# Norms behind three output projections taken in halves of the tokens, and an opening that waits for each x tile by itself

## The chip, the cores and the metric

One core of a Trainium2 chip runs the whole program. The metric is the device time of one execution in microseconds, taken as the median of the runs shown. Times inside an execution come from one profiled execution and count from the start of its span.

## The reference

Two transformer stages over one batch of 512 tokens of width 1024, all in float32. The first stage is a hybrid layer; the second has two layers whose norms are scaled and shifted by a vector computed from a condition, with an FFN that has a three-tap convolution over the tokens. For this change these lines matter (the second stage's norms have the form `norm(x) * (1 + scale) + shift`, and its branches are multiplied by a gate row before they are added):

```python
def rms_norm(x, g):
    x32 = x.astype(jnp.float32)
    y = x32 * lax.rsqrt(jnp.mean(x32 * x32, axis=-1, keepdims=True) + EPS) * g.astype(jnp.float32)
...
x = x + 0.5 * swiglu(rms_norm(x, ffn1_norm), ffn1_w_in, ffn1_w_out)
...
x = x + mix @ w_mix_out
x = x + 0.5 * swiglu(rms_norm(x, ffn2_norm), ffn2_w_in, ffn2_w_out)
```

## The kernel before

**Numbers.** Each float32 operand is split into a high and a low float32r part, and each product is made of three matmuls: high by high, low by high, high by low (`feature_major`, L344 to L346, and `token_major`, L350 to L352). Weights come in chunks of up to 128 x 2048, in two slots that alternate: SP loads `raw` (`load`, L340), ScalarE writes `w_hi` (`split_hi`, L323), VectorE writes `w_lo` (`split_lo`, L327). Chunks are numbered through the program. ScalarE may write `w_hi` of a chunk only when TensorE has used up the chunk two before it; SP may load a chunk when VectorE has split the one two before it.

**Order of work.** Each engine runs one list of instructions in program order, written out by hand in the blocks at the end of the file; semaphores join them. Stages: `norm_ffn1`, `ffn1`, `norm_mix`, the mixer's projection, attention, `out_1`; `norm_ffn2`, `ffn2`; then twice a layer of projection, attention, output projection (`out_2`, `out_3`), norm and FFN (`ffn3`, `ffn4`); a final norm.

**Norm.** `x` lies as four token tiles of 128 x 1024. For each, `stats_act` (L589, L591) squares and sums on ScalarE and takes the root, `scale_dve` (L597, L599) scales on VectorE into another tile, and TensorE transposes it in 128 x 128 blocks (L671) into PSUM. One PSUM bank holds feature tile t of all 512 tokens, so the bank is complete only with the last token tile. ScalarE then writes `xT_hi` (L617; with a shift L624 and L627) and VectorE `xT_lo` (L643; with a shift L646, and L654 for the odd tiles' scaling). `part(t)` lets a reader wait for feature tile t.

**FFN.** The hidden width is done in two halves of 11 tiles. In each there are ten tiles in pairs of slots (a pair is a gate tile and an up tile, 48 matmuls of 512 columns, one chunk), one single tile, and then the output matmuls in four chunks for each half of the columns, accumulated by token tile in banks 4 to 7. The halves and the pairs are loops. The first tile of a pair waits for `part(kt)` of the norm. After a pair, VectorE multiplies and splits the result (L902, L905). In `ffn1` VectorE also computes the modulation vector, eight steps (L546) for every two pairs, from weights that POOL loads into four slots; each step frees a slot for the next load. `ffn3` and `ffn4` apply the convolution (L832, L894).

**MixOut.** Two panels of 512 output columns; each has two chunks (pieces) of four k-tiles, and each piece goes over the four token tiles with 12 matmuls for each. A panel is done piece by piece: all tokens of piece 0, then all tokens of piece 1, so the token tiles become complete within the last 48 matmuls. VectorE adds the tiles to `x` as they complete (L2092, with a gate row L2094 and L2097) and scales the one before. The next FFN's first chunk is split by the FFN's predecessor in the ordinary order, ahead of the last adds. Between the panels of `out_2` stand the transposes and copies of a gate row (L2030, L2036, L2037) and on VectorE and ScalarE the sines and cosines (`rope_dve`, L2181 to L2194; `rope_act`, L2198).

**Opening.** SP loads the norm's vector, the four x tiles (one semaphore, x_in, that must reach 64), the first chunk, some 30 small vectors (`constants_load`, L377) and then the other chunks. TensorE transposes the vectors (`constants_pe`, L449 to L452, into banks 2 and 3) behind the norm's tile 3 and ahead of the first pair. VectorE copies them (`constants_dve`, L471 to L473) and makes two bias strips (L477 to L491), which POOL stores (`strips_store`) after six panels of modulation weights.

## Time and profile before

| | |
|---|---|
| median of 3 runs | 2290.57 us (2290.14 to 2291.48) |
| the profiled execution's own time | 2297.45 us |
| its span | 2295.9 us |
| mean granted clock of TensorE | 0.984 |
| TensorE idle, 2295.9 - 2219.4 busy | 76.5 us |
| ScalarE and VectorE busy | 952.0 and 1270.2 us |
| SP's issues of the small vectors, first to last | 4.15 to 19.3 us |
| ScalarE, the longest chunk's w_hi; VectorE, its w_lo | 1.9 and 2.29 us |

How to read it: an engine's row says when an instruction began and how long it was busy. Instructions of TensorE overlap, so the distance between two starts is the pace, and the duration shown is longer. "Idle before" names what ended the engine's wait. A granted clock of 1 is 2.4 GHz and 0.5 is 1.2 GHz; a number between is a mean over the stretch.

### The profile page before, as it was taken

How to read it: one execution, taken by the hardware profiler on the slowest of the kernel's cores; microseconds unless marked ns; L12 is line 12 of the kernel's file. 1: busy time of each engine (PE TensorE's matmuls, PEld its weight loads, DVE VectorE, ACT ScalarE, POOL GpSimd, SP SyncE). 2: the span in 40 equal slices, each digit the busy share in tenths (PEclk: the TensorE clock that was granted, in tenths of full speed). 3: DMA queues.
4: the chain of work that ended last, by engine and by line, in shares of the span. 5: the costliest groups of instructions: out<-in, count | busy, mean ns of one | idle time of the engine just before them, and what ended most of it. 6: DMA issues, size and time to landing. Idle time of an engine off the chain costs nothing.

```text
span 2295.9 us, 31127 instructions
## 1 busy us (share of the span) xinstructions
PE 2219.4 (97%) x11504; PEld 1829.6 (80%) x11504; DVE 1270.2 (55%) x2069; ACT 952.0 (41%) x1464; POOL 266.7 (12%) x442
## 2 busy tenths in 40 slices
PE   7999999998999999999999999999989999999998
PEld 5888887977778888887878788888878887888886
DVE  5754764455743363355347666456376755644554
ACT  4222223356734323324237454244254755533542
POOL 2110220034400020011027000000000430000000
PEclk9999999998999999999999999999999999999999
DMA  7863983231033274264221232332312212323332
GB/s 232 278 221 111 317 300 96 92 103 38 11 110 93 85 254 140 77 233 142 92 91 44 74 105 78 111 99 73 103 46 83 65 38 73 91 92 100 91 96 87
DMA packets 259489, 267.97 MB, mean 117 GB/s; under 512 B 9111, under 2 KB 202174, under 8 KB 259406
## 3 DMA queue, kind: packets, MB, share of 16 engines
q1 hardware_dynamic: 237677, 188.25, 27.6%
q0 software_dynamic: 21728, 78.63, 10.1%
q8 instruction: 50, 0.82, 0.1%
q14 instruction: 34, 0.27, 0.0%
HBM read 263.62 MB, written 12.66 MB: 120 GB/s over the span
## 4 chain that ended last, share of the span: by engine, by line
PE 88%; DVE 5%; ACT 4%; POOL 1%; issue 1%; DMA 1%; DVEq 0%; SPq 0%; ACTq 0%; POOLq 0%
PE bank L344 16%; PE bank L345 16%; PE bank L346 15%; PE bank L350 11%; PE bank L351 11%; PE bank L352 11%; PE bank L1571 2%; PE bank L1546 2%; PE bank L1522 2%; POOL probs L1729 1%; ACT probs L1607 1%; DVE w_lo L327 1%; DVE xT_lo L646 1%; PE bank L671 1%; PE bank L1945 0%
## 5 line engine op out<-in xcount | busy, mean ns | idle before, releaser
L327 DVE TENSOR_TENSOR w_lo<-raw,w_hi 128x2048 fp32r<-128x2048 f32 (+3 forms) x202 | 415.5, 2057 | 377.3 <-ACT w_hi L323 374.6
L344 PE MATMUL bank<-xT_hi,w_hi 128*128 128x512 f32 x1560 | 609.9, 391 | 5.1 <-DVE xT_lo L646 4.3
L345 PE MATMUL bank<-xT_lo,w_hi 128*128 128x512 f32 x1560 | 608.0, 390 | 0.0
L346 PE MATMUL bank<-xT_hi,w_lo 128*128 128x512 f32 x1560 | 607.8, 390 | 0.0
L323 ACT ACTIVATE w_hi<-raw 128x2048 fp32r<-128x2048 f32 (+3 forms) x202 | 348.2, 1724 | 485.7 <-PE bank L352 430.8
L344 PEld LDWEIGHTS bank<-xT_hi,w_hi 128*128 128x128 f32 x1560 | 292.7, 188 | 72.3 <-DVE xT_lo L646 8.2
L346 PEld LDWEIGHTS bank<-xT_hi,w_lo 128*128 128x128 f32 x1560 | 292.7, 188 | 62.1
L345 PEld LDWEIGHTS bank<-xT_lo,w_hi 128*128 128x128 f32 x1560 | 292.8, 188 | 60.3
L350 PE MATMUL bank<-w_hi,hid_hi 128*128 128x512 f32 x704 | 277.8, 395 | 0.0
L351 PE MATMUL bank<-w_lo,hid_hi 128*128 128x512 f32 x704 | 277.8, 395 | 0.0
L352 PE MATMUL bank<-w_hi,hid_lo 128*128 128x512 f32 x704 | 277.7, 395 | 0.0
L1729 POOL TENSOR_SCALAR probs<-probs,stat 128x256 f32<-128x256 f32 (+2 forms) x120 | 113.6, 958 | 726.6 <-DVE stat L1642 696.2
L840 ACT ACTIVATE hid_hi<-act_u 128x512 f32 (+1 forms) x88 | 55.6, 632 | 296.0 <-DVE act_u L902 296.0
L352 PEld LDWEIGHTS bank<-w_hi,hid_lo 128*128 128x128 f32 x704 | 132.7, 188 | 31.0
L350 PEld LDWEIGHTS bank<-w_hi,hid_hi 128*128 128x128 f32 x704 | 132.6, 188 | 31.0
L351 PEld LDWEIGHTS bank<-w_lo,hid_hi 128*128 128x128 f32 x704 | 132.7, 188 | 30.9
L1607 ACT ACTIVATE probs<-probs,small 128x512 f32<-128x512 f32 (+2 forms) x224 | 120.9, 542 | 63.6 <-DVE small L1671 63.6
L894 DVE SCALAR_TENSOR_TENSOR act_u<-bank,cols,act_u 128x511 f32<-128x511 f32 x88 | 65.9, 749 | 79.2 <-ACT act_u L832 72.8
L350 PE MATMUL bank<-w_hi,xT_hi 128*128 128x512 f32 (+2 forms) x288 | 102.5, 356 | 3.0 <-DVE xT_lo L646 2.9
L832 ACT ACTIVATE act_u<-bank,cols 128x512 f32<-128x512 f32 x44 | 34.3, 780 | 166.3 <-PE bank L346 166.3
L905 DVE TENSOR_TENSOR hid_lo<-act_u,hid_hi 128x512 f32 (+1 forms) x88 | 60.9, 692 | 76.0 <-ACT hid_hi L840 76.0
L351 PE MATMUL bank<-w_lo,xT_hi 128*128 128x512 f32 (+2 forms) x288 | 101.3, 352 | 0.0
(306 smaller groups left out, 2845.4 us busy)
## 6 DMA issues: line engine op xcount, KB each, us to landing
raw<-in_ffn_w_in_dram SPq DMA_DIRECT2D x40, 1024.0 KB, 6.2
raw<-in_f_win_dram SPq DMA_DIRECT2D x40, 1024.0 KB, 6.1
mod_w<-in_mod_w_dram POOLq DMA_DIRECT2D x48, 512.0 KB, 5.4
mod_w_more<-in_mod_w_dram POOLq DMA_DIRECT2D x48, 512.0 KB, 5.8
raw<-in_ffn_w_out_dram SPq DMA_DIRECT2D x24, 768.0 KB, 4.5
raw<-in_f_wout_dram SPq DMA_DIRECT2D x24, 768.0 KB, 4.4
raw<-in_a_wqkv_dram SPq DMA_DIRECT2D x12, 1024.0 KB, 5.2
skewed_strips<-bias_strips POOLq DMA_DIRECT2D x32, 320.0 KB, 6.6
```

Of the source, the lines that this page charges most:

```text
L323: act.activation(w_hi[:, slot, :n], raw[:, slot, :n], ACT.Copy).then_inc(hi_done, 1)
L327: dve.tensor_tensor(out=w_lo[:, slot, :n], in0=raw[:, slot, :n], in1=w_hi[:, slot, :n].bitcast(f32), op=ALU.subtract).then_inc(lo_done, 1)
L344: pe.matmul(o, lhsT=w[0], rhs=xs[0], start=first, stop=False)
L345: pe.matmul(o, lhsT=w[0], rhs=xs[1], start=False, stop=False)
L346: return pe.matmul(o, lhsT=w[1], rhs=xs[0], start=False, stop=last)
L350: pe.matmul(o, lhsT=xs[0], rhs=w[0], start=first, stop=False)
L351: pe.matmul(o, lhsT=xs[0], rhs=w[1], start=False, stop=False)
L352: return pe.matmul(o, lhsT=xs[1], rhs=w[0], start=False, stop=last)
L894: dve.scalar_tensor_tensor(out=dst[:, u, shift:], in0=bank[b][:, :SEQ - shift], scalar=w, in1=dst[:, u, shift:], op0=ALU.mult, op1=ALU.add ...
L905: dve.tensor_tensor(out=hid[1], in0=act_u[:, u, :], in1=hid[0].bitcast(f32), op=ALU.subtract).then_inc(pair_free[u], 1)
L1607: act.activation(p, p, ACT.Exp, scale=-1.0, bias=self.least(k, i), accum_out=self.sums(k, i)).then_inc(self.e, 1)
L1729: return engine.tensor_scalar(p, p, self.inverses(k, i), None, ALU.mult)
```

## The change

In the opening each x tile gets a semaphore of its own; ScalarE runs one square root on a constant first (`root_table`); the second chunk of weights is loaded ahead of the small vectors; eight extra 128 x 128 matmuls stand in front of the last feature tile's transposes of the first norm; the vectors' transposes move behind pair 0 of `ffn1` and into banks 4 and 5, their copies in front of pair 0's product on VectorE, and the strips' work into the first output stage (`strips_dve`).

The norms behind `out_1`, `out_2` and `out_3` become `HalfNorm`. The last panel is done in the order: piece 0 and piece 1 of token tiles 0 and 1, piece 0 of tiles 2 and 3, the transposes of tiles 0 and 1, piece 1 of tiles 2 and 3. A bank then holds two feature tiles of 256 tokens. ScalarE and VectorE write `xT_hi` and `xT_lo` for half the tokens at a time (`half_act`, `half_dve`). The FFN's pair 0 is done in two parts of 256 columns (`by_halves`), with the second half's transposes between them. The first FFN chunk is split between the statistics of tiles 0, 1 and half 0; its second chunk's w_hi (`second_split`) comes in front of half 1. In `out_2` the panel's second chunk is split ahead of the sines, and `modulate_for` comes ahead of the last panel's adds. The loops over an FFN's halves are written out, with pairs 0 and 1 of the first half ahead of the loop.

The core of the diff (the changes of counters, of calls and of the loops' frames are left out):

```diff
-        in_dma, x_in, first_in, small_in = sem("in_dma"), sem("x_in"), sem("first_in"), sem("small_in")
+        in_dma, first_in, small_in = sem("in_dma"), sem("first_in"), sem("small_in")
+        x_in = [sem(f"x_in{s}") for s in range(TOK)]
...
-            pe.transpose(bank[3][:, 0:P], rows[:, 4, :], ident[:, :])
+                pe.transpose(bank[4][:, b * P:(b + 1) * P], rows[:, b, :], ident[:, :])
+            pe.transpose(bank[5][:, 0:P], rows[:, 4, :], ident[:, :])
...
+        def strips_dve(dve):
             dve.wait_ge(small_in, 16 * SMALL_INS)
...
+        def first_tiles_dve(dve):
+            constants_dve(dve)
+            dve.wait_ge(cond_done, 1)
...
+        def root_table(act):
+
+            act.wait_ge(lo_done, 2)
+            act.activation(stat[:, 0:1], eps[:, :], ACT.Sqrt)
...
+                    if self.n == 0 and t == KT - 1:
+                        for _ in range(BUSY):
+                            pe.matmul(self.banks[t][:, 0:P], lhsT=ident[:, :], rhs=ident[:, :], start=True, stop=True)
...
+            def __init__(self, ready, gains, shifts=None, places=((4, 5, 2, 3), (6, 7, 4, 5))):
+                super().__init__(ready, gains, shifts)
+                self.places = [[bank[b] for b in half] for half in places]
...
+            def half_pe(self, pe, h):
+                for s in (2 * h, 2 * h + 1):
+                    pe.wait_ge(n_xn, self.n + s + 1)
+                    for t in (0, 2, 1, 3, 4, 6, 5, 7):
+                        ins = pe.transpose(self.place(h, t)[:, s % 2 * P:(s % 2 + 1) * P], self.tile(s)[:, t * P:(t + 1) * P],
+                                           ident[:, :])
+                        if s % 2 and t // 2 % 2:
+                            ins.then_inc(n_T, 1)
...
+            def shifted_by_act(self, h, t):
+
+                return h == 0 and t < 4
...
+            def half_act(self, act, h, ts):
+                for t in ts:
+                    hi = xT_hi[:, t, PAIR * h:PAIR * (h + 1)]
+                    if self.shifts is None:
+                        act.wait_ge(n_T, self.t + 4 * h + self.bank_of(t) + 1)
+                        if t // 2 % 2:
+                            self.part(act, t - 2, h)
+                        act.activation(hi, self.place(h, t), ACT.Identity, scale=self.gains[:, t:t + 1],
+                                       bias=zero[:, :]).then_inc(n_hi, 1)
+                        continue
+                    if t % 2 == 0 or self.shifted_by_act(h, t):
+                        act.wait_ge(n_T, self.t + 4 * h + self.bank_of(t) + 1)
+                        self.shift_free(act, h, t)
+                        act.activation(self.shifted(t), self.place(h, t), ACT.Identity, scale=self.gains[:, t:t + 1],
+                                       bias=self.shifts[:, t:t + 1]).then_inc(n_full[t % 2], 1)
+                    act.wait_ge(n_full[t % 2], self.f + 4 * h + t // 2 + 1)
+                    act.activation(hi, self.shifted(t), ACT.Copy).then_inc(n_hi, 1)
...
+            def end_act(self, act, split, gained, second):
+
+                for s in range(2):
+                    self.stats_act(act, s)
+                split(act)
+                if gained is not None:
+                    act.wait_ge(*gained)
+                self.half_act(act, 0, range(4))
+                self.stats_act(act, 2)
+                self.half_act(act, 0, range(4, KT))
+                self.stats_act(act, 3)
+                second(act)
+                self.half_act(act, 1, range(KT))
+
+            def end_dve(self, dve, add, split):
+                for s in range(2):
+                    add(s)
+                for s in range(2):
+                    self.scale_dve(dve, s)
+                split(dve)
+                self.half_dve(dve, 0, range(4))
+                for s in range(2, TOK):
+                    add(s)
+                self.half_dve(dve, 0, range(4, KT))
+                for s in range(2, TOK):
+                    self.scale_dve(dve, s)
+                self.half_dve(dve, 1, range(KT))
...
+                def by_halves():
+
+                    pe.wait_ge(lo_done, self.pair_c(0, 0, 0) + 1)
+                    pe.wait_ge(pair_free[0], EVEN * 2 * self.n + 1)
+                    for part in range(2):
+                        if part:
+                            self.norm.half_pe(pe, 1)
+                        for kt in range(KT):
+                            self.norm.part(pe, kt, part)
+                            for b, done in enumerate((g_done, used)):
+                                last = feature_major(pe, bank[b][:, PAIR * part:PAIR * (part + 1)],
+                                                     w_part(self.slot(0), (b * KT + kt) * P, P),
+                                                     xT_part(kt, PAIR * part, PAIR), kt == 0, kt == KT - 1)
+                                if part and kt == KT - 1:
+                                    last.then_inc(done, 1)
+
+                def half(h, first=False):
+                    if first:
+                        if self.norm.parts == 2:
+                            by_halves()
+                        else:
+                            pair(h, 0, 0)
+                        if between:
+                            between(pe)
+                        pair(h, 0, 1)
...
+            def second_split(self, act):
+                split_hi(act, self.pair_c(0, 0, 0) + 1, self.slot(1), self.land(1, 0))
...
+                def one(h, i, u, between=None, split=True):
                     c = self.pair_c(h, i, u)
-                    split_hi(act, c + 1, self.slot(u + 1), self.land(u + 1, PER_HALF // 2 * h + i))
+                    if split:
...
+                            if later and np == 0 and q == 1:
+                                later(dve)
...
+            def pe(self, pe, norm, between=None):
                 self.gemm.piece(pe, 0, 0, [2, 3])
                 self.gemm.piece(pe, 0, 1, range(TOK))
                 if between:
                     between(pe)
-                self.gemm.pe(pe, 1)
+                self.gemm.piece(pe, 1, 0, [0, 1])
+                self.gemm.piece(pe, 1, 1, [0, 1])
+                self.gemm.piece(pe, 1, 0, [2, 3])
+                norm.half_pe(pe, 0)
+                self.gemm.piece(pe, 1, 1, [2, 3])
...
+            def act(self, act, norm, second, row=None, later=None, gained=None):
+                self.gemm.split_act(act, 0)
+                if row:
+                    row(act)
+                c = self.gemm.panels[1][3]
+                next_hi(act, c)
+                if later:
+                    later(act)
+                norm.end_act(act, lambda act: next_hi(act, c + 1), gained, second)
...
+                self.gemm.split_dve(dve, 0)
+                for s in range(TOK):
+                    add(0, s)
+                c = self.gemm.panels[1][3]
+                next_lo(dve, c)
+                if between:
+                    between(dve)
+                if modulate:
+                    modulate(dve)
+                norm.end_dve(dve, lambda s: add(1, s), lambda dve: next_lo(dve, c + 1))
...
-            ffn1.pair_sp(sp, 0, 0, 0)
+                sp.dma_start(x[:, s, :], A["x"][0, s * P:(s + 1) * P, :]).then_inc(x_in[s], 16)
+            for u in range(2):
+                ffn1.pair_sp(sp, 0, 0, u)
             constants_load(sp)
...
-            norm_ffn1.act(act, None, lambda act: split_hi(act, 2, 0, landed(2)))
+            root_table(act)
+            norm_ffn1.act(act, (cols_done, 1), lambda act: split_hi(act, 2, 0, landed(2)))
...
-            dve.wait_ge(cond_done, 1)
-            ffn1.dve(dve)
+            ffn1.dve(dve, first_tiles_dve, strips_dve)
...
-            norm_ffn1.part(pe, 3)
-            constants_pe(pe)
-            ffn1.pe(pe)
+            ffn1.pe(pe, constants_pe)
```

## Rows read from the trace of the kernel before

**Rows 1.** The page, part 1: busy us, share of the span, instructions.

```profile
PE 2219.4 (97%) x11504; PEld 1829.6 (80%) x11504; DVE 1270.2 (55%) x2069; ACT 952.0 (41%) x1464; POOL 266.7 (12%) x442
```

**Rows 2.** Waits of TensorE, whole span: us in total, times, longest.

```profile
PE bank L671 <- DVE xn L599: 17.5, 7, 10.2
```

**Rows 3.** Landing of the x tiles (issues 1.53 to 2.84), first chunk (issue 3.36).

```profile
DMA to landing us min/median/max: 3.6/5.0/6.3
...
raw<-in_ffn_w_in_dram SPq DMA_DIRECT2D x1, 1024.0 KB, 10.2
```

**Rows 4.** Timeline of the opening: start us, us, engine, line, operation.

```profile
9.16 1.06 ACT L589 ACTIVATE xn<-x 128x1024 f32<-128x1024 f32 x1 [4.68 <-DMA x<-in_x_dram]
...
11.82 1.04 ACT L589 ACTIVATE xn<-x 128x1024 f32<-128x1024 f32 x1
...
15.92 1.90 ACT L323 ACTIVATE w_hi<-raw 128x2048 fp32r<-128x2048 f32 x1
...
17.85 2.29 DVE L327 TENSOR_TENSOR w_lo<-raw,w_hi 128x2048 fp32r<-128x2048 f32 x1 [0.85 <-ACT w_hi L323]
...
20.06 5.35 DVE L643 SCALAR_TENSOR_TENSOR xT_lo<-bank,cols,xT_hi 128x512 fp32r<-128x512 f32 x8
...
24.28 1.08 PE L449 MATMUL bank<-ident,rows 128*128 128x128 f32 x4 [3.20 <-DVE xT_lo L643]
...
33.01 0.39 PE L344 MATMUL bank<-xT_hi,w_hi 128*128 128x512 f32 x1
...
36.41 0.39 PE L344 MATMUL bank<-xT_hi,w_hi 128*128 128x512 f32 x1
...
39.50 0.69 DVE L902 TENSOR_TENSOR act_u<-act_g,bank 128x512 f32<-128x512 f32 x1 [6.06 <-PE bank L346]
```

**Rows 5.** Stretches: busy us of each engine, then granted clock, DMA share, GB/s.

```profile
25.90:31.00 5.10, 5.10 (x14) 4.01 (x14) 4.71 (x28) 1.91 (x1) 0.00 (x0) 0.53 0.68 172
...
1919.00:1922.00 3.00, 3.00 (x17) 3.00 (x16) 2.34 (x4) 2.64 (x5) 0.00 (x0) 0.56 0.00 0
```

**Rows 6.** Timeline of VectorE, the first modulation transfer that it waits for.

```profile
57.20 1.23 DVE L546 CUSTOM_DVE_ANT_0 mod_w_more<-mod_w_more,c_row 128x1024 f32<-128x1024 f32 x1 [2.23 <-DMA mod_w_more<-in_mod_w_dram]
```

**Rows 7.** Timeline, projection to FFN 2: panel's first matmul, first transposes, pair 0's product.

```profile
655.38 0.40 PE L350 MATMUL bank<-w_hi,q_hi 128*128 128x512 f32 x1
...
677.78 1.03 PE L671 MATMUL bank<-ident,xn 128*128 128x128 f32 x8
...
694.75 0.69 DVE L902 TENSOR_TENSOR act_u<-act_g,bank 128x512 f32<-128x512 f32 x1 [2.14 <-PE bank L346]
```

**Rows 8.** Timeline of TensorE in the mixer's projection: matmuls of 256 columns.

```profile
431.73 0.28 PE L350 MATMUL bank<-w_hi,xT_hi 128*128 128x256 f32 x1
...
433.40 0.28 PE L352 MATMUL bank<-w_hi,xT_lo 128*128 128x256 f32 x1
```

**Rows 9.** Timeline, projection to FFN 4: panel's first matmul, pair 0's last product read.

```profile
1891.27 0.47 PE L350 MATMUL bank<-w_hi,q_hi 128*128 128x512 f32 x1 [1.27 <-ACT row L2037]
...
1934.78 0.78 ACT L832 ACTIVATE act_u<-bank,cols 128x512 f32<-128x512 f32 x1 [3.49 <-PE bank L346]
```

**Rows 10.** Groups by line and form, 256 columns: count, busy us, mean ns, idle before.

```profile
L1254 ACT ACTIVATE k_hi<-bank,zero,cols 128x256 fp32r<-128x256 f32 x4 | 2.3, 568 | 0.0
...
L2279 DVE TENSOR_SCALAR full<-bank,stat 128x256 f32<-128x256 f32 x4 | 1.9, 484 | 0.1
```

**Rows 11.** Timeline, projection to FFN 3: rope's first and last operation, panel, pair 0's end.

```profile
1276.46 0.42 DVE L2181 CAST ang<-ang 128x512 f32<-128x512 int32 x1
...
1277.23 0.47 PE L350 MATMUL bank<-w_hi,q_hi 128*128 128x512 f32 x1 [1.26 <-ACT row_early L2037]
...
1283.64 0.49 DVE L2194 TENSOR_SCALAR sin<-sin,cols 128x512 f32<-128x512 f32 x1 [1.22 <-ACT cos L2199]
...
1321.14 0.78 ACT L832 ACTIVATE act_u<-bank,cols 128x512 f32<-128x512 f32 x1 [3.51 <-PE bank L346]
```

**Rows 12.** The page, part 5: a group of weight loads.

```profile
L344 PEld LDWEIGHTS bank<-xT_hi,w_hi 128*128 128x128 f32 x1560 | 292.7, 188 | 72.3 <-DVE xT_lo L646 8.2
```

189 lines of the change are left out of this document (105 added, 84 removed).

## The prediction

> **What bounds the kernel now.** I read the page's first part: TensorE is busy 97% of the span [rows 1], so almost any gain must come out of the 76.5 us in which it idles or out of stretches in which its work is done at a lower clock. The waits of TensorE come next: the longest in total is that of the norm's transposes (L671) for the scaled tiles, 17.5 us, of which 10.2 us is the opening [rows 2]. Then I read the timeline around the opening and around the three places where an output projection (MixOut) is followed by a norm and an FFN. In each I measure one stretch: from the first matmul of the projection's second panel to the end of the FFN's first pair.
>
> **Opening.** Before, ScalarE's statistics start at 9.16, when the last of four x tiles has landed (the semaphore counts all four); the four landed 3.6 to 6.3 us after their issues at 1.53 to 2.84 [rows 3]. The chunk of weights landed 10.2 us after its issue at 3.36, so at 13.6 [rows 3]. The order is then: statistics until 15.9 with a table load between the first and the second, w_hi 1.90, w_lo 2.29, eight xT_lo from 20.06 in 5.35, the constants' transposes at 24.28, pair 0 until 39.5 [rows 4]. From 25.9 to 31.0 the granted clock is 0.53 [rows 5]: after an idle 3.2 us TensorE is at 1.2 GHz, and pair 0 takes 13.4 us (from 26.0) instead of the 48 x 0.227 = 10.9 that full clock gives; 0.227 is (36.41 - 33.01)/15 [rows 4].
>
> After, statistics start with tile 0 at 1.53 + 3.6 = 5.1 and repeat every 1.37 us (11.82 to 15.92 for three [rows 4]); the table load lies before them, beside the transfer. They end at 5.1 + 4 x 1.37 = 10.6. What is late next is the weights' chunk at 13.6, which costs the change 3 us of the 5 that it frees. w_hi runs 13.6 to 15.5, w_lo to 17.8, the xT_lo from there, 0.67 each, until 23.2. TensorE starts pair 0 at 18.5, a tile behind. Its gate tile is paced by the xT_lo (0.67 against 3 x 0.227 = 0.68), so pair 0 ends at 18.5 + 10.9 = 29.4, if the clock is full; the constants' transposes behind it (seven, 0.8) let pair 1 start at 30.2. Before it started at 39.3. That is **9.1 us**. The idle stretch before pair 0 is short: the transposes of t 4 to 7 with the eight added ones fill 12 to about 16.4, which leaves 2.1 us against the 3.2 that preceded the slow stretch.
>
> Given back: constants_dve (1.2 us of copies) now stands in front of pair 0's product, so the DVE's modulation steps run 1.0 us later relative to pair 1. Before, the DVE waited 2.2 us for a modulation transfer at 57.20 and the next w_lo was thereby 0.7 late [rows 6]; now 1.7. I take 1.0 off: **8.1 us**. On SP the second chunk stands in front of some 30 small constants' loads. It needs its own landing only by 23 (w_hi after c_row's Silu); the constants must land by 29.4. Their issues took from 4.15 to 19.3; behind another 1 MB (some 4 us at the rate of the opening) they end near 23 to 28, so they are covered, barely: bounds 0 and 4 us. I take 0. The strips' work, 4.2 us at most between 26.9 and VectorE's next split, moves into an output stage, where a chunk of three k-tiles keeps TensorE 36 x 0.233 = 8.4 us and asks one split of VectorE (2.29 at most). POOL's strips_store comes only after six modulation panels. Between 0 and 4.2 I take 0.
>
> **Projection to FFN 2.** The panel's 96 matmuls run from 655.38 to 677.78, 0.233 each; pair 0 ended at 694.75 [rows 7]: 39.4 us. The least that TensorE needs is 22.4 for the panel, 3.5 for 32 transposes (eight take 1.03 with the tail of the last, so about 0.11 each), and pair 0 in halves. Pair 0 becomes 96 matmuls of 256 columns; such matmuls follow each other at (433.40 - 431.73)/14 = 0.119 us [rows 8], 11.5 us instead of 10.9, so 0.6 dearer. The Trainium skill, "TensorE: Matmul & The Clock Gate", section "Back-to-back issue gap", has it that a matmul costs its columns at 2.4 GHz and 2.5 ns; by that the halving costs 0.1 us a stretch and not 0.6, 1.5 us less in all. The row decides, and the sum keeps 0.6.
>
> Floor 37.4, so at most 2.0 to gain. Let T be 11.2 us into the panel, when its first two quarters have completed token tiles 0 and 1; times in this part count from T. ScalarE and VectorE finish adds (0.69, as the operation of [rows 7]), statistics (1.37) and scaling of tiles 0 and 1 by 3.2; TensorE goes on with a quarter until 5.6, transposes half 0 until 7.4, then the last quarter until 13.0. The weights' split waits for the slot freed at 5.6: w_hi to 7.6, w_lo to 10.0 and only then half 0's xT_lo, four by 11.8; adds of tokens 2 and 3 to 13.8; four more xT_lo to 16.1. TensorE runs part 0 from 13.0 to 18.8 without a gap, since it needs t = 4 at 15.9. Tokens 2 and 3 are scaled by 18.1. Half 1: transposes to 20.6, first xT_lo at 20.9, part 1 until 26.7. Total 11.2 + 26.7 = 37.9: 39.4 - 37.9 = **1.5 us** gained.
>
> **Projection to FFN 4** (gate and shift). First matmul 1891.27, the pair's end 1934.78 [rows 9]: 43.5 us, the transposes in part at a granted clock of 0.56 [rows 5]. After: a shifted tile of 256 columns costs ScalarE 0.57 for the scaling, and VectorE 0.48 an operation [rows 10]; the copy costs ScalarE 0.40 (1.90 at 2048 columns and 1.04 at 1024 [rows 4] give 0.84 ns a column). Half 0's first four tiles are all on ScalarE, to 11.6, the adds (two operations of 0.69 each) to 14.6, four more tiles to 17.7, scaling to 19.8, transposes to 20.7. Half 1 in pairs of tiles: 0.57 + 0.40 + 0.40 + hand-offs = 1.5 us, four pairs, last xT_lo at 27.2, part 1's end at 27.9. VectorE splits the second chunk only behind half 1: 27.2 + 2.29 = 29.4. Pair 1 thus starts at 11.2 + 29.4 = 40.6, 1.5 us after pair 0's end; this wait is late next. Before, pair 1 had its weights in time. Gain 43.5 - 40.6 = **2.9 us**; floor 37.4, so at most 6.1.
>
> **Projection to FFN 3.** First matmul 1277.23, pair's end 1321.14 [rows 11]: 43.9. As above, but the rope work stands in front of the adds. It took 1276.46 to 1284.13 on VectorE; now the split of the panel's second chunk precedes it (w_hi from 1277.1, w_lo to 1281.3, needed at 1277.2 + 5.6 = 1282.8, in time), so it ends at 1289.0, 0.6 after T = 1288.4, and modulate_for(1) follows it. The adds then start 0.9 late, and TensorE, which wants half 0 at T + 5.6, waits 1.0 for token 1. 43.9 - 40.6 - 0.9 = **2.4 us**.
>
> **Sum.** 8.1 + 1.5 + 2.4 + 2.9 = 14.9. The profiled execution took 2297.45 (span 2295.9), 6.9 above the median of the three runs; its work is the same, so I take the difference off both: 2297.45 becomes 2282.6, the median 2290.57 becomes 2275.7. A run of this kernel can tell 0.2%, 4.6 us, from no change.
>
> **Rivals.** (a) *Opening half as good.* TensorE enters pair 0 at 1.2 GHz after its idle 2.1 us. In the trace it did so after 3.2 us idle and was low for some 6 us (24.3 to 31.0, less what the mean of 0.53 leaves for full clock); the same again costs 3 us, and late constants can cost as much. For: at FFN 4, where bursts of transposes alternate with waits, the clock fell too [rows 5]. Against: the idle is shorter, and the eight extra transposes lengthen the dense stretch. The time is 2275.7 + 3 = 2279, 2282 with both. The Trainium skill, "TensorE: Matmul & The Clock Gate", section "What's actually happening", has the low clock as the default that activity lifts; by that rule an opening that idles before pair 0 is this rival, 2279. (b) *The halves do not do what they say.* VectorE works in order: w_lo, then tiles, then adds, and the hand-offs between two engines cost more than I allow. A chain 3 us longer in each of three stretches takes all of 6.8: 2290.57 - 8.1 = 2282.5. For: the second chunk's split already ends behind pair 0. Against: the slack of 3 us before token 2's scaling. (c) *Better than forecast.* The stretches come near their floors (2.0, 6.5 and 6.1 instead of 1.5, 2.4 and 2.9) and the modulation wait does not grow: 9.1 and some 11 of these 14.6 make 20: 2270. (d) *Slower.* Matmuls of 256 columns are paced by their weight load. A load is busy 0.188 us [rows 12]; were that the pace, each pair in halves would take 96 x 0.188 = 18.0 instead of 11.5, 0.069 more for each of 288, 19.9 in all: 2275.7 + 19.9 = 2295.6. It decides from a pace of 0.119 + 14.9/288 = 0.171. The projection's own rows at 0.119 speak against it.
>
> **How the numbers follow.** Forecast 0.45, (a) 0.25, (b) 0.15, (c) 0.12, (d) 0.03. The range runs from 2268 (c, with 2 us more from the bounds) to 2284 (b, with some of a). Faster by more than 0.2% (below 2286): all of the first four but a tail of (a) and (b) together, 0.93; same 0.04; slower 0.03, from (d).
>
> **What the profile would show.** Right: statistics from 5.1 with no table load between them; w_hi waiting for its transfer at 13.6; pair 0 from 18.5, at 0.227 a matmul; constants' transposes behind pair 0 near 29.4; in each stretch 16 transposes between the third and the last quarter and no TensorE wait above 1 us in FFN 2's; in FFN 3's and 4's a wait of 1.5 for w_lo behind pair 0. Wrong: a granted clock near 0.5 at pair 0, a wait for the rows' DMA in front of L449, xT_lo of half 0 later than TensorE's last quarter, matmuls of 256 columns above 0.13.

## The result and the profile after

The changed kernel takes 2276.76 us (median of 5 runs, 2274.81 to 2282.02), the kernel before 2291.48 in the same series (2290.14 to 2294.35): ratio 0.9938, interval 0.9925 to 0.9952. The forecast was 2275.7, with a range of 2268 to 2284. The profiled execution took 2276.76, its span is 2275.1, and its mean granted clock 0.990 against 0.984.

The page, part 1, of the kernel after (busy us, share, instructions), and two of TensorE's waits over the whole span (total, times, longest):

```profile
PE 2211.4 (97%) x11664; PEld 1830.0 (80%) x11664; DVE 1273.5 (56%) x2097; ACT 897.2 (39%) x1455; POOL 268.1 (12%) x442
```

```profile
PE bank L683 <- DVE xn L611: 12.0, 8, 4.4
...
PE bank L344 <- DVE xT_lo L786: 2.1, 3, 0.9
```

Against [rows 1], TensorE is busy 8 us less with 160 instructions more: 144 from the three pairs in halves, and the eight added in the opening, which count twice (L699, x16). Fewer busy microseconds for more instructions is the mark of a higher clock, but most of that is not the change's: the kernel before, run and profiled once more (before_again, below), was busy 2212.9 us and idle for 76.0. What the change took away is idle time, from 76.5 to 63.7. Of the 17.5 us that the transposes waited for scaled tiles [rows 2], 12.0 are left: the opening's 10.2 became 4.4, and the half transposes (L741) wait only 0.3 in all.

**Opening.** Timeline of the kernel after, the lines that answer to [rows 4, 6]:

```profile
1.05 1.28 ACT L517 ACT_TABLE_LOAD   x1 [1.05 <-PEq L2953]
...
4.72 1.06 ACT L601 ACTIVATE xn<-x 128x1024 f32<-128x1024 f32 x1 [2.17 <-DMA x<-in_x_dram]
...
8.75 1.06 ACT L601 ACTIVATE score<-x 128x1024 f32<-128x1024 f32 x1 [0.85 <-DMA x<-in_x_dram]
...
13.56 0.63 PE L683 MATMUL bank<-ident,xn 128*128 128x128 f32 x2
...
14.48 1.91 ACT L323 ACTIVATE w_hi<-raw 128x2048 fp32r<-128x2048 f32 x1 [2.87 <-DMA raw<-in_ffn_w_in_dram]
...
16.12 2.39 PE L699 MATMUL bank<-ident 128*128 128x128 f32 x16
...
18.35 0.38 PE L683 MATMUL bank<-ident,xn 128*128 128x128 f32 x2
...
18.64 5.35 DVE L655 SCALAR_TENSOR_TENSOR xT_lo<-bank,cols,xT_hi 128x512 fp32r<-128x512 f32 x8
...
19.52 0.47 PE L344 MATMUL bank<-xT_hi,w_hi 128*128 128x512 f32 x1 [0.58 <-DVE xT_lo L655]
...
30.52 0.60 PE L450 MATMUL bank<-ident,rows 128*128 128x128 f32 x4
...
31.40 0.50 PE L344 MATMUL bank<-xT_hi,w_hi 128*128 128x512 f32 x1
```

The order is the predicted one: table load beside the transfer, statistics from 4.72, ScalarE then waiting 2.87 us for the chunk, pair 0 behind the first xT_lo, the constants behind pair 0. The chunk landed at 14.4 and not at 13.6 [rows 3], and everything after it is 0.9 to 1.2 late against the forecast: pair 1 at 31.40, forecast 30.2, 39.13 before. The chunk's issue at 3.36 and its time to landing:

```profile
raw<-in_ffn_w_in_dram SPq DMA_DIRECT2D x1, 1024.0 KB, 11.1
```

This time scatters from one execution to the next. It is 9.8 to 11.4 us in the eight profiles with the second chunk issued right behind the first, and 9.9 to 11.0 in the six without, so the second chunk is not shown to delay it. The scatter passes straight on: in the six profiles that have the whole of the new opening (in the table below, with second_split_ordinary and attention_filled), pair 1 starts 16.9 to 17.0 us after the landing, although its start moves between 30.14 and 31.52. The landing is what limits this opening.

The idle time ahead of pair 0 is 0.58 us, not the 2.1 of the forecast. The transposes came later than forecast and went at half pace at first: two of them took 0.43 us at 13.56 and 0.22 at 18.35. (The granted clock of these early stretches reads 1.00 all the same; ahead of some 17 us it is not to be trusted.) In pair 0 clock and pace agree on full speed (stretches as in [rows 5]):

```profile
18.00:20.00 2.00, 1.42 (x11) 1.18 (x10) 2.00 (x4) 2.00 (x4) 0.00 (x0) 1.00 1.04 395
20.00:22.00 2.00, 2.00 (x10) 1.62 (x10) 2.00 (x5) 1.98 (x4) 0.00 (x0) 1.00 1.04 398
```

**The three stretches.** TensorE in the kernel after, FFN 2 first, then FFN 3 and FFN 4 [rows 7, 11, 9]: a stretch's panel, transposes, first and last matmul of part 0, part 1, pair 1.

```profile
640.80 0.40 PE L350 MATMUL bank<-w_hi,q_hi 128*128 128x512 f32 x1
...
657.60 1.91 PE L741 MATMUL bank<-ident,xn 128*128 128x128 f32 x16
...
664.93 0.28 PE L344 MATMUL bank<-xT_hi,w_hi 128*128 128x256 f32 x1
...
670.56 0.28 PE L346 MATMUL bank<-xT_hi,w_lo 128*128 128x256 f32 x1
670.68 1.91 PE L741 MATMUL bank<-ident,score 128*128 128x128 f32 x16
...
673.11 0.39 PE L344 MATMUL bank<-xT_hi,w_hi 128*128 128x256 f32 x1 [0.52 <-DVE xT_lo L783]
...
679.44 0.50 PE L344 MATMUL bank<-xT_hi,w_hi 128*128 128x512 f32 x1 [0.32 <-DVE w_lo L327]
...
1262.54 0.47 PE L350 MATMUL bank<-w_hi,q_hi 128*128 128x512 f32 x1 [1.27 <-ACT row_early L2209]
...
1280.83 1.09 PE L741 MATMUL bank<-ident,xn 128*128 128x128 f32 x8 [0.27 <-DVE xn L611]
...
1302.66 0.50 PE L344 MATMUL bank<-xT_hi,w_hi 128*128 128x512 f32 x1 [0.74 <-DVE w_lo L327]
...
1873.98 0.47 PE L350 MATMUL bank<-w_hi,q_hi 128*128 128x512 f32 x1 [1.26 <-ACT row L2209]
...
1906.73 0.39 PE L344 MATMUL bank<-xT_hi,w_hi 128*128 128x256 f32 x1 [0.91 <-DVE xT_lo L786]
...
1913.47 0.50 PE L344 MATMUL bank<-xT_hi,w_hi 128*128 128x512 f32 x1 [0.74 <-DVE w_lo L327]
```

Pair 1's first matmul in the kernel before, in the same three places:

```profile
694.36 0.39 PE L344 MATMUL bank<-xT_hi,w_hi 128*128 128x512 f32 x1
...
1320.77 0.39 PE L344 MATMUL bank<-xT_hi,w_hi 128*128 128x512 f32 x1
...
1934.42 0.39 PE L344 MATMUL bank<-xT_hi,w_hi 128*128 128x512 f32 x1
```

From the panel's first matmul to pair 1's: 38.6 (forecast 37.9, before 39.0), 40.1 (forecast 41.5, before 43.5) and 39.5 (forecast 40.6, before 43.2). So the stretches are 0.3, 3.4 and 3.7 us shorter. The prediction's 39.4, 43.9 and 43.5 for the kernel before run on to the first reading of pair 0's product, some 0.4 later.

A part of the last two gains is the clock. Before, TensorE fell to 1.2 GHz for a while among these transposes, in FFN 4's stretch as [rows 5] show and in FFN 3's here; in the kernel after, each of the three stretches has a granted clock of 1.00.

```profile
1303.00:1308.00 5.00, 3.95 (x23) 3.80 (x22) 3.37 (x6) 2.95 (x6) 0.00 (x0) 0.66 0.01 3
```

Matmuls of 256 columns follow each other at (670.56 - 664.93)/47 = 0.120 us. The weight load does not pace them; rival (d) is out. The Trainium skill, "TensorE: Matmul & The Clock Gate", section "Back-to-back issue gap", gives for an isolated matmul its columns at 2.4 GHz and 2.5 ns, an estimate of 0.109 us by its formula; here, with a weight load for each, the trace shows 0.120, and the measurement decides.

### The profile page after: what moved, and what is told of

Same layout as the page of the kernel before. It is cut to its first block, busy times and chain, and to the rows that moved or that the text cites. A ratio compares the mean times of both kernels' runs of the same rounds, so it can differ in the third digit from the quotient of the medians.

```text
span 2275.1 us, 31047 instructions
## 1 busy us (share of the span) xinstructions
PE 2211.4 (97%) x11664; PEld 1830.0 (80%) x11664; DVE 1273.5 (56%) x2097; ACT 897.2 (39%) x1455; POOL 268.1 (12%) x442
## 3 DMA queue, kind: packets, MB, share of 16 engines
q8 instruction: 63, 1.03, 0.2%
## 4 chain that ended last, share of the span: by engine, by line
PE 87%; DVE 5%; ACT 4%; DMA 2%; POOL 1%; issue 1%; SPq 0%; DVEq 0%; ACTq 0%; POOLq 0%
PE bank L344 15%; PE bank L345 15%; PE bank L346 15%; PE bank L350 11%; PE bank L352 11%; PE bank L351 11%; PE bank L1743 2%; PE bank L1718 2%; PE bank L1694 2%; DMA raw<-in_ffn_w_in_dram 1%; POOL probs L1901 1%; ACT probs L1779 1%; DVE w_lo L327 1%; ACT w_hi L323 1%; DVE probs L1843 0%
## 5 line engine op out<-in xcount | busy, mean ns | idle before, releaser
L344 PE MATMUL bank<-xT_hi,w_hi 128*128 128x512 f32 (+1 forms) x1608 | 617.9, 384 | 7.2 <-DVE w_lo L327 2.3
L346 PE MATMUL bank<-xT_hi,w_lo 128*128 128x512 f32 (+1 forms) x1608 | 615.9, 383 | 0.0
L345 PE MATMUL bank<-xT_lo,w_hi 128*128 128x512 f32 (+1 forms) x1608 | 615.9, 383 | 0.0
L344 PEld LDWEIGHTS bank<-xT_hi,w_hi 128*128 128x128 f32 x1608 | 301.5, 188 | 71.3 <-DVE w_lo L327 3.7
L346 PEld LDWEIGHTS bank<-xT_hi,w_lo 128*128 128x128 f32 x1608 | 301.6, 188 | 60.0
L345 PEld LDWEIGHTS bank<-xT_lo,w_hi 128*128 128x128 f32 x1608 | 301.6, 188 | 58.6
```

Of the source, the lines that this page charges most:

```text
L344: pe.matmul(o, lhsT=w[0], rhs=xs[0], start=first, stop=False)
L345: pe.matmul(o, lhsT=w[0], rhs=xs[1], start=False, stop=False)
L346: return pe.matmul(o, lhsT=w[1], rhs=xs[0], start=False, stop=last)
```

## The experiments

The times are medians with the ratio to the kernel before of the same series. A second reading is steadier than they are: VectorE's fourth add of a projection's first panel stands at the same place in every version, so the spans between these adds of out_1, out_2 and out_3 can be compared across kernels. In us, from each one's profile:

| kernel | pair 1's first matmul | add in out_1 | to out_2 | to out_3 | to the end |
|---|---|---|---|---|---|
| before | 39.13 | 655.58 | 620.27 | 614.04 | 406.0 |
| before_again | 36.77 | 647.46 | 621.36 | 613.90 | 406.2 |
| opening_alone | 30.64 | 639.31 | 621.46 | 613.84 | 406.2 |
| halves_alone | 37.61 | 648.86 | 619.88 | 611.39 | 402.5 |
| after | 31.40 | 641.00 | 620.17 | 611.44 | 402.5 |
| after_again | 31.18 | 646.07 | 620.19 | 610.89 | 402.5 |
| pair0_whole | 30.83 | 646.34 | 625.69 | 616.01 | 407.4 |

**opening_alone**: the changed kernel with before's projections, norms and first pairs.

```diff
-        norm_ffn2 = HalfNorm(out_1.x_ready, column("ffn2_norm", KT))
+        norm_ffn2 = Norm(out_1.x_ready, column("ffn2_norm", KT))
...
-        norm_ffn3 = modulated_half_norm(1, out_2.x_ready)
+        norm_ffn3 = modulated_norm(1, out_2.x_ready)
```

> The opening of the change with the three output projections, norms and first pairs as before. Prediction's theory: the opening is worth 8.1 us (ratio 0.9965, about 2283 against 2291), and the trace of the changed kernel, in which pair 1 starts at 31.4 instead of 39.3, says 7.9. Rival: part of it is given back behind, because VectorE has the constants' copies in front of pair 0's product and its modulation steps come later: then 7 or less (0.997), and a wait of TensorE for w_lo (L327) between 50 and 60 us would show it.

**halves_alone**: the other part alone.

```diff
-        norm_ffn1 = Norm(lambda s: [(x_in[s], 16)], column("ffn1_norm", KT))
+        norm_ffn1 = Norm(lambda s: [(x_in[k], 16) for k in range(TOK)] + [(cols_done, 1)], column("ffn1_norm", KT))
...
-        BUSY = 8
+        BUSY = 0
...
-            root_table(act)
...
-            ffn1.pe(pe, constants_pe)
+            norm_ffn1.part(pe, 3)
+            constants_pe(pe)
+            ffn1.pe(pe)
```

> The halves with the opening as before (statistics wait for all four x tiles, no square root ahead, no added matmuls, constants transposed ahead of pair 0 and copied and made into strips ahead of it, second chunk loaded behind the constants). Prediction's theory: 1.5 + 2.4 + 2.9 = 6.8 us, about 2284 (0.9970). By the stretches of the changed kernel's trace: 0.8 + 3.8 + 4.0 = 8.6, about 2282 (0.9962). Rival: the halves hand back later what they gain, since VectorE ends their stretches without slack: 4 or less (over 0.998). The two parts alone should sum to the whole change, 14.7.

opening_alone took 2282.29 (0.9961, 0.9948 to 0.9975), halves_alone 2283.2 (0.9963, 0.9950 to 0.9977). The product of the ratios is 0.9924; the whole change measured 0.9938 and, again, 0.9939, which the intervals allow. The table says where each part acts: the opening before out_1 alone, the halves behind it alone. The opening's gain at the add in out_1 is the mean of before_again and halves_alone, 648.16, less that of opening_alone and after, 640.16: 8.0. The halves gain 0.9, 2.7 and 3.6 in the last three columns (means of the three kernels without them less those of the three with them): 7.2. Together 15.2, and the parts do not disturb each other. Only the 0.9 is doubtful: in that column the kernels without the halves differ by 1.2 among themselves.

The expectation for halves_alone put 8.6 us on the stretches; by ends that are alike they give 0.3 + 3.4 + 3.7 = 7.4, close to the table's 7.2.

**before_again** and **after_again**: both kernels unchanged, once more.

> The kernel before, unchanged. Theory A: the 6.9 us by which its profiled execution stood above its median are a stretch at low clock at the start of the attention (between 500 and 530 us) that comes in some executions: a profile that lies near the median has a granted clock near 1 there and passes from pair 1's start to the output projection's panel in about 609 us instead of 616. Theory B: it is what profiling costs this kernel: the new profile is some 6 us above the median again. Ratio 1.000 either way, within 0.001.

> The changed kernel once more. Theory: its times scatter as those of the kernel before do, by how long TensorE stays at 1.2 GHz at the start of the first attention (32 matmuls on cmp_w in 3.8 to 4.2 us, or in 6.9), so a part of the runs lies near 2282 and above at a mean clock of 0.985 to 0.987 and the rest near 2276 at 0.990; the ratio to the kernel before is 0.994, within 0.0015. Rival: the five runs taken first were all it does, and the ratio depends on which share of slow starts each kernel has: then this series may differ by 0.003 with the same code.

before_again took 2292.27 (1.0001, 0.9991 to 1.0011), with its profiled execution at 2290.39; after_again 2279.23 (0.9939, 0.9921 to 0.9956; 2276.17 to 2284.35), with its at 2281.29. So profiling costs nothing that shows, and one code is 7 us apart from itself. The timeline of the first attention's 32 small matmuls says where most of it lies; one line each of before, before_again, after and after_again:

```profile
513.97 6.93 PE L1945 MATMUL bank<-cmp_in,cmp_w 128*128 128x62 f32 x32
```

```profile
511.10 3.84 PE L1945 MATMUL bank<-cmp_in,cmp_w 128*128 128x62 f32 x32
```

```profile
504.45 4.02 PE L2117 MATMUL bank<-cmp_in,cmp_w 128*128 128x62 f32 x32
```

```profile
504.54 6.93 PE L2117 MATMUL bank<-cmp_in,cmp_w 128*128 128x62 f32 x32
```

TensorE enters this attention with short gaps and drops to 1.2 GHz; in some executions it stays there through these 32 matmuls. Between 505 and 515 us the granted clock is 0.99 in the kernel after and 0.50 in after_again. From pair 1 to the add in out_1 the long kind takes 614.1 to 616.5 us and the short kind 608.7 to 611.3. Of the fourteen profiles, those with 6.2 to 6.9 us here have a mean clock of 0.983 to 0.988, those with 3.8 to 4.2 one of 0.986 to 0.990. Like against like, the spans give 2295.9 - 2279.6 = 16.3 where both were long, and 2288.9 - 2275.1 = 13.8 where both were short.

**no_added_matmuls**: `BUSY = 0`.

> The changed kernel without the eight matmuls on the identity in front of the first norm's last tile. Theory that they keep TensorE at full clock: without them TensorE idles from about 16.1 until its last tile's transposes near 16.5 and then until 19.5, the granted clock in pair 0 falls to between 0.5 and 0.9 and pair 1 starts at about 34.4 instead of 31.4, as after the idle 3.2 us of the kernel before: 3 us slower (2280). Rival: the transposes themselves end close enough to pair 0 that the clock stays at 1: pair 1 at 31.4 or up to 2 us sooner where the added matmuls were in the way, 2276.8 or less.

2278.72 (0.9940, 0.9924 to 0.9957), which the times can't tell from the change. The trace can: TensorE's first matmul of pair 0, and the stretches (granted clock is the third number from the end) of this kernel:

```profile
19.85 0.77 PE L344 MATMUL bank<-xT_hi,w_hi 128*128 128x512 f32 x1 [2.94 <-DVE xT_lo L655]
```

```profile
18.00:20.00 2.00, 0.15 (x1) 0.18 (x2) 2.00 (x3) 2.00 (x5) 0.00 (x0) 0.92 1.03 404
20.00:22.00 2.00, 2.00 (x5) 1.61 (x6) 2.00 (x4) 2.00 (x4) 0.00 (x0) 0.50 1.05 397
22.00:24.00 2.00, 2.00 (x8) 1.54 (x8) 2.00 (x4) 1.97 (x3) 0.00 (x0) 0.73 0.92 315
```

After 2.94 us idle, TensorE runs the first eight matmuls of pair 0 near 1.2 GHz, 0.43 apart instead of 0.23, and pair 1 starts at 33.25, 1.85 later. Of this, 0.3 is a later landing of the chunk (11.4 us instead of 11.1); pair 0 and the vectors' transposes take 13.4 us instead of 11.9, and these 1.5 us are what the added matmuls buy. They leave 0.58 us of idle time ahead of pair 0 instead of 2.94. By the rule of the Trainium skill, "TensorE: Matmul & The Clock Gate", section "What's actually happening", the low clock is the default and activity lifts it; this run and the one with them agree.

**x_waits_together**: all four x tiles waited for at once, as before.

```diff
-        norm_ffn1 = Norm(lambda s: [(x_in[s], 16)], column("ffn1_norm", KT))
+        norm_ffn1 = Norm(lambda s: [(x_in[k], 16) for k in range(TOK)] + [(cols_done, 1)], column("ffn1_norm", KT))
```

> The changed kernel, but the first statistics wait for all four x tiles, as before. Prediction's theory: the four statistics (4 x 1.37) then run from 8.8 or 9.2 to 14.6, where the chunk of weights lands at 14.4 too, so the transposes come 3 us later but w_hi hardly at all; xT_lo follow w_lo at 18.7 only if tiles 0 to 3 are transposed by then, and they are (from 15.6, 16 in 1.8). Pair 1 starts at 31.4 + 0 to 1: of the 7.9 us the semaphores would be worth 1 or less, since the chunk's landing is the limiter. Rival: the statistics are the chain, and pair 1 comes 3 us later, 34.4 (2279.8).

2279.45 (0.9940, 0.9918 to 0.9962). Pair 1 starts at 33.35, 1.95 later, which looks like a value between both expectations. But in this execution the chunk landed early, 10.0 us after its issue, at 13.4; the changed kernel would have had pair 1 at 13.4 + 16.9 = 30.3 then. So waiting for all x tiles costs 3 us, as the rival had it, and here the statistics are the limit and not the chunk: w_hi starts only at 14.96, 1.6 behind the landing. The rest is a wait that neither expectation named. The transposes end late, and the last tile stands behind the added matmuls, so that ScalarE waits for it:

```profile
21.74 0.78 ACT L629 ACTIVATE xT_hi<-bank,zero,cols 128x512 fp32r<-128x512 f32 x1 [0.20 <-PE bank L683]
```

Pair 0's first matmul is queued behind these transposes, at 21.46. That the added matmuls are good only where x is early is likely by this, but this kernel was not run without them.

**constants_first**: before's place for the vectors, on SP, TensorE and VectorE.

```diff
-            for u in range(2):
-                ffn1.pair_sp(sp, 0, 0, u)
+            ffn1.pair_sp(sp, 0, 0, 0)
             constants_load(sp)
+            ffn1.pair_sp(sp, 0, 0, 1)
...
-            ffn1.pe(pe, constants_pe)
+            norm_ffn1.part(pe, 3)
+            constants_pe(pe)
+            ffn1.pe(pe)
```

> The changed kernel with the constants' part of the opening as before: second chunk loaded behind the small vectors, their transposes (banks 2 and 3) ahead of pair 0, their copies ahead of pair 0's product on VectorE; strips still late. Prediction's theory: TensorE waits for the vectors' rows, whose last issue is at about 19.3 to 20, so the transposes come at 21.5 to 22 instead of pair 0 at 19.5: pair 0 from 22.6, pair 1 at 33.6, and the second chunk, issued behind them at 20 and 9 us to landing, 29, gives w_lo at 33.4, about in time: 2 to 3 us slower than the changed kernel (2279). Rival: the rows have landed by 19.5, and only 0.8 us moves from behind pair 0 to ahead of it: nothing (2276.8).

2282.84 (0.9956, 0.9938 to 0.9973), 4 us above the change by the ratios and more than expected. Its timeline, VectorE and TensorE:

```profile
18.58 5.35 DVE L655 SCALAR_TENSOR_TENSOR xT_lo<-bank,cols,xT_hi 128x512 fp32r<-128x512 f32 x8
```

```profile
23.50 0.64 PE L450 MATMUL bank<-ident,rows 128*128 128x128 f32 x4 [4.42 <-DVE xT_lo L655]
```

The name behind the wait is wrong, and the times show it: TensorE needs the first four xT_lo, and they were done by 18.58 + 4 x 0.67 = 21.3. It waited until 23.50 for what is left of its conditions, the vectors' rows, whose last issues SP made from 17.92 on. Then pair 0 starts at 24.63 at 1.2 GHz, and pair 1 at 36.95, where the kernel before has it (36.77 to 39.13). The chunk had landed as in the changed kernel (11.0 and 11.1 us). So with x early and the table loaded, the vectors' place alone (in SP's order, TensorE's and VectorE's) keeps the opening where it was: it is the largest piece of this part, 5.5 us. The pieces are not a sum: taken back one at a time, they cost 5.5, 3 and 1.5, and the whole part is worth 6.9 at pair 1. The vectors' move without the rest was not run. The same lines of before read likewise: xT_lo from 20.06, four by 22.7, the vectors' transposes at 24.28 [rows 4].

**opening_shorter** and **opening_shorter_pool**: what the opening still leaves.

```diff
             ffn1.pair_sp(sp, 0, 0, 0)
+            sp.wait_ge(raw_landed[0], 16)
             ffn1.pair_sp(sp, 0, 0, 1)
...
+                self.evacuate_act(act, range(2 if between else 0))
                 if between:
                     between(act)
-                self.evacuate_act(act, range(KT))
+                self.evacuate_act(act, range(2 if between else 0, KT))
...
+            pool.wait_ge(raw_landed[0], 16)
             pool.dma_start(c_row[:, :], A["c_2"][0].partition_broadcast(P)).then_inc(cond_in, 16)
```

(VectorE is edited as ScalarE; the last two lines are in opening_shorter_pool alone.)

> The changed kernel with two edits that follow from reading its opening: SP issues the second chunk only when the first has landed, and ScalarE and VectorE make xT_hi and xT_lo of feature tiles 0 and 1 ahead of the weights' split, in the 2.9 us in which ScalarE waited for the chunk. Theory (the chunk's landing at 14.4 and then w_hi, w_lo, first xT_lo are the chain): the chunk shares the DMA engines with less and lands 0.8 to 1.5 us sooner, the first xT_lo is done before w_lo, 0.7: pair 1 at 29.2 to 29.9 instead of 31.4, 1.5 to 2.2 us faster (about 2275), which a trace shows and the times hardly. Rival: the small vectors are now issued from 14 to 33 us and land after pair 0's end: TensorE waits for them and pair 1 starts at 34 or later.

> The same, and POOL issues c_row and the first modulation weights (2.5 MB) only when the first chunk has landed. Theory that bandwidth sets the chunk's landing: 1 us sooner still than in the run above. Rival: they were issued from 11.3 on, too late to delay the chunk much, and coming 2 us later they make VectorE's modulation steps wait longer, a w_lo near 50 us comes late and TensorE waits 1 to 2 us for it.

2279.77 (0.9953, 0.9931 to 0.9975; 2276.69 to 2289.91) and 2280.68 (0.9935, 0.9915 to 0.9955). Pair 0 starts at 18.13, 1.4 sooner, and the gain is lost at its end, as the rival had it:

```profile
30.25 0.66 PE L450 MATMUL bank<-ident,rows 128*128 128x128 f32 x4 [0.94 <-DMA rows<-in_mod_b_dram]
```

Pair 1 starts at 31.18, 0.2 sooner. With POOL held back too it starts at 32.17. The chunk took 10.3 and 10.6 us to land, within the scatter of the kernels that leave SP and POOL alone (9.8 to 11.4), so neither edit is shown to make it land sooner. Counted from this landing, pair 0 starts 4.5 us behind it in opening_shorter and 5.1 in the changed kernel: the new order of ScalarE and VectorE gains 0.6. But pair 1 comes 17.5 us behind the landing instead of 16.9, and 18.2 with POOL held back, so the late vectors cost more than that. Neither kernel can be told from the change by its time, and no version here is shown to beat it.

**pair0_whole**: half 1 transposed first, then pair 0 in one.

```diff
-                    for part in range(2):
-                        if part:
-                            self.norm.half_pe(pe, 1)
-                        for kt in range(KT):
...
+                    self.norm.half_pe(pe, 1)
+                    for kt in range(KT):
+                        self.norm.part(pe, kt, 1)
+                        for b, done in enumerate((g_done, used)):
+                            last = feature_major(pe, bank[b][:, :], w_part(self.slot(0), (b * KT + kt) * P, P),
+                                                 xT_part(kt), kt == 0, kt == KT - 1)
```

> The changed kernel, but behind the last quarter TensorE transposes half 1 first and then runs pair 0 whole, 48 matmuls of 512 columns, instead of part 0, transposes, part 1. Prediction's theory: what the halves bring is that part 0 (5.8 us) runs while ScalarE and VectorE finish half 1. Without it TensorE idles from T + 13 until half 1's first xT_lo near T + 20.9 and then needs 10.9 us, to T + 31.8 instead of 26.7: about 5 us a stretch, 4.3 in FFN 3 and 4 where a wait of 0.7 behind pair 0 is covered, 13.5 in all: 2290, as slow as the kernel before or slower. Rival: the reordered panel and the half's early transposes carry the gain, and 256 columns cost 0.6 more a pair: then 2 us a stretch or less, 2277 to 2283.

2293.07 (1.0001, 0.9991 to 1.0012): as slow as the kernel before, with the opening's gain still in it. The last three columns of the table grow by 5.6, 4.8 and 4.9 over the mean of the three kernels with the halves. TensorE's waits of this kernel, whole span, and its longest in the timeline:

```profile
PE bank L741 <- DVE score L611: 15.7, 3, 5.8
```

```profile
1918.99 3.65 PE L741 MATMUL bank<-ident,score 128*128 128x128 f32 x16 [5.79 <-DVE score L611]
```

Three idle stretches of 4.7 to 5.8, after which the 16 transposes take 3.65 instead of 1.91 at the lower clock. The halves live by part 0 lying over half 1's norm, and the reordered panel without it loses.

**second_split_ordinary**: the second chunk's w_hi behind half 1.

```diff
                 self.stats_act(act, 3)
-                second(act)
...
-                        one(h, 0, 0, None, self.norm.parts == 1)
+                        one(h, 0, 0)
```

> The changed kernel with the second chunk's w_hi behind half 1 on ScalarE, in the FFN's ordinary order. Theory from the changed kernel's trace: ScalarE is then free 1.9 us sooner for half 1, whose first xT_lo had been waited for by 0.5 to 0.9; but w_hi comes at the end of half 1 (1910.6 to 1912.5 in FFN 4's stretch) and w_lo ends at 1914.8 instead of 1913.4, so pair 1 starts 1.3 us later in each of three stretches: 4 us slower, 2281. Rival: half 1 ends so much sooner (1.5 us) that it pays for it: no difference.

2281.88 (0.9962, 0.9945 to 0.9980). Half 1's first wait is 0.91 as before the edit, so ScalarE's split was not what delayed it, and pair 1 waits longer (1.32 in FFN 2, in FFN 4 the line below, 1.35 more than with the change). The early split is worth 1.0 to 1.35 a stretch by the wait alone. In FFN 4 the longer wait also cost the clock: the span from the add in out_3 to the end is 405.5 us instead of 402.5, 3.0 more, and behind the 2.09 us of idle time the granted clock is 0.53, as the second line shows. Whether that comes in every execution is not shown.

```profile
1914.74 0.51 PE L344 MATMUL bank<-xT_hi,w_hi 128*128 128x512 f32 x1 [2.09 <-DVE w_lo L327]
```

```profile
1916.00:1919.00 3.00, 3.00 (x9) 2.33 (x8) 2.36 (x4) 0.87 (x2) 0.00 (x0) 0.53 0.85 251
```

**attention_filled**: nine matmuls on the identity in the first attention's first gaps.

```diff
+                        for _ in range(self.fill.get(k - 1, 0)):
+                            pe.matmul(bank[4][:, 0:P], lhsT=ident[:, :], rhs=ident[:, :], start=True, stop=True)
                         self.transposes_pe(pe, k - 1)
...
+        att_1.fill = {0: 5, 1: 1}
```

> The changed kernel with nine matmuls of 128 columns on the identity put into TensorE's first gaps of the first attention (three ahead of the gates' transposes, five ahead of the first and one ahead of the second transposes of probabilities). In the changed kernel's trace the granted clock there falls to 0.5 at about 495 and is back at 504.8; in the profiled execution of the kernel before it stayed low over 32 matmuls that took 6.9 us instead of 3.8. Theory: as in the opening, filled gaps keep the clock: the stretch 494 to 506 is 4 to 5 us shorter, and the times, which scatter by this, lie closer together at the low end: 2272. Rival: the fill itself takes as long as it saves, or the clock falls a little later anyway: 2276 to 2278, with runs at 2282 still among them.

2280.88 (0.9947, 0.9932 to 0.9961). No gain, as the rival had it, though the time is above its 2276 to 2278: TensorE still falls to 1.2 GHz at 495, is back at 498.5, goes on faster than the scaling of probabilities can follow, waits four times (0.33 to 0.46) and falls again at the 32 matmuls:

```profile
503.47 0.44 PE L1724 MATMUL bank<-ident,probs 128*128 128x128 f32 x2 [0.46 <-POOL probs L1907]
504.37 0.44 PE L1724 MATMUL bank<-ident,probs 128*128 128x128 f32 x2 [0.46 <-POOL probs L1907]
504.64 6.20 PE L2123 MATMUL bank<-cmp_in,cmp_w 128*128 128x62 f32 x32
```

## Why the prediction was right, and where its steps were off

- **The sum.** 14.9 was forecast, 14.7 is the difference of the medians, and the profiles give 8.0 + 7.2 = 15.2. The forecast's terms were 8.1 for the opening and 6.8 for the halves, and each part alone confirms its own, by the table more closely than by the times. The mechanisms are the ones forecast. That the terms came so close is in part luck, since errors inside both cancel, as the next points show.
- **The opening's 9.1.** Pair 1 at 30.2 was 1.2 too early. "What is late next is the weights' chunk at 13.6" was right as a mechanism: pair 1 follows the landing by 16.9 us, where the forecast's own steps give 16.6. The rest is the landing itself, read from one execution and scattering by 1.6. The place it was measured from was off too: pair 1 before starts at 36.77, 37.61 or 39.13, by when the vectors' rows land. I had read that wait as one for xT_lo, as the profile names it, and so took the constants' move for order and cover, priced at nothing, when it is the largest piece (constants_first). The six profiles with the new opening lie between 30.14 and 31.52, mean 30.95, the three with the old one at 37.84: 6.9 by pair 1's start.
- **The 1.0 given back.** It did not come, and the sign was wrong: at the add in out_1 the opening is worth 8.0, 1.1 more than at pair 1. The wait for the modulation transfer was forecast to make w_lo 1.7 us late; TensorE does not wait there at all, where it waited 0.70 (before) and 1.03 us (before_again). VectorE's copies did take their 1.0, and the pairs that now stand outside the loop gave it back: see below. So 9.1 less 1.0 was forecast and 6.9 plus 1.1 came: two errors of some 2 us that cancel.
- **FFN 2, 1.5 forecast.** (T is 11.2 us into the panel, as in the prediction.) By the stretch 0.3, by the table an unsure 0.9. Of the missing 1.2, 0.4 is the forecast's end for the kernel before, which lies behind pair 1's start. The step that failed is "part 1 until 26.7": I had left out that VectorE's second split comes behind half 1 in this stretch too (w_lo until T + 27.4), and part 1 began at T + 21.1, not 20.9.
- **FFN 3 and FFN 4, 2.4 and 2.9 forecast.** By the stretches 3.4 and 3.7, by the table 2.7 and 3.6. The wait for w_lo behind pair 0 is there, as named, with 0.74 instead of 1.5. In FFN 4 VectorE finished half 1 at T + 25.9 where I had 27.2: four pairs of tiles took 1.43 each instead of 1.5 and started at T + 20.2, a microsecond sooner than 27.2 less four times 1.5. In FFN 3 the rope's delay made the stretch 0.6 longer than FFN 4's and not 0.9 (TensorE's wait for a scaled tile is 0.27 of it); the rope ended at 1274.1, 0.4 behind T. From the add in out_2 to the last hid_lo of FFN 3 it is 340.7 us before and 337.3 after, so all of the 3.4 is still there; 0.8 of it is gone behind the attention that follows. A longer low clock does not explain that: the granted clock over the 60 us concerned is 0.91 in both (1650 to 1710 after, 1665 to 1725 before). It stays open.
- **The own time of the profile.** The 6.9 us taken off both sides was right: most of it is the length of the low clock in the first attention, which either kernel may meet.
- **Rivals.** (a) is a real mechanism that the added matmuls keep away: without them it costs 1.5, not 3. With the 2.1 us of idle time that the forecast had ahead of pair 0 it might have come (2.09 us were followed by a fall in second_split_ordinary); it was 0.58. (b), (c) and (d) did not come.

## What to carry to other kernels

A norm between two matmul stages can be hidden in halves of the tokens, but only if the next stage also starts on the half that is ready; reordering the producer alone loses. In an opening, ask of each wait which of its conditions really came last: a batch of thirty small loads can hold the first pair while the profile names the engine beside it. Compare profiles between fixed places in the program, and with like ends, since one stretch that wavers can hide or feign a gain of 0.2%. Where a transfer's landing limits a stretch, count from the landing: it scattered here by 1.6 us, as much as the added matmuls are worth.

## What the runs showed of the hardware that was not expected

**Instructions outside a loop hand over sooner.** VectorE's product and hid_lo of a first pair, in before_again and in the kernel after (where that pair's code is written out; the number in brackets is the wait between them):

```profile
38.75 0.69 DVE L905 TENSOR_TENSOR hid_lo<-act_u,hid_hi 128x512 f32 x1 [0.93 <-ACT hid_hi L840]
...
57.14 2.29 DVE L327 TENSOR_TENSOR w_lo<-raw,w_hi 128x2048 fp32r<-128x2048 f32 x1 [0.36 <-issue]
```

```profile
33.82 0.69 DVE L1065 TENSOR_TENSOR hid_lo<-act_u,hid_hi 128x512 fp32r<-128x512 f32 x1 [0.70 <-ACT hid_hi L992]
...
50.94 2.29 DVE L327 TENSOR_TENSOR w_lo<-raw,w_hi 128x2048 fp32r<-128x2048 f32 x1
```

0.23 less a pair, and from the last modulation step's start (55.17 and 49.44) to w_lo 1.97 against 1.50: together 0.9 over two pairs, which is what kept w_lo in time. halves_alone tells the two apart, since in it ScalarE's first pairs are written out and VectorE's are still in the loop:

```profile
39.49 0.69 DVE L1065 TENSOR_TENSOR hid_lo<-act_u,hid_hi 128x512 f32 x1 [0.82 <-ACT hid_hi L992]
...
56.69 2.29 DVE L327 TENSOR_TENSOR w_lo<-raw,w_hi 128x2048 fp32r<-128x2048 f32 x1 [0.36 <-issue]
```

The hand-off is halfway, 0.82, and the 0.36 is still there. So the hand-off has a share from each engine's loop, and the 0.36 ahead of w_lo, the first instruction of a pass, goes with VectorE's own. Whether it is the loop's addresses, its branch or something else is not shown.

**The low clock has no one price.** 2.94 us idle cost 1.5; 2.09 us idle was followed by a granted clock of 0.53 and some 1.6; 5.8 us idle cost 1.74 on 16 transposes alone; gaps of 1.4 us or less, in the first attention, cost 0.2 to 0.5 or 3.2 on the same 32 matmuls (3.84 to 4.2 or 6.93, against 3.68 at full clock), from one execution to the next.
